# Paired projection: low parts of the weights by accumulating transfers, sums of tokens on VectorE, sums of squares on ScalarE

## The chip, the cores and the metric

One core of one Trainium2 chip runs the kernel. The metric is the time of one execution in microseconds of the device: 2842.64 us is the median of three runs, the lowest 2840.53, the highest 2844.08.

## What is computed

Two layers of a hybrid decoder on a sequence of 1024 tokens with 1024 features, all in float32. In a layer the normalised input goes through one wide projection w_in; its columns feed a retention branch of 4 heads and a gated delta-rule branch of 8 heads, and the gates. Both branches are lifted, gated, added and projected back onto the input.

```python
proj = h @ w_in
qkv = jax.nn.silu(causal_conv(jnp.concatenate([dq, dk, dv], axis=-1), conv_w))
dq = l2norm(dq) * (DN_DK ** -0.5); dk = l2norm(dk)
o_d = gated_deltanet(dq, dk, dv, beta, g)      # chunked, with a triangular solve in each chunk
o_d = o_d * lax.rsqrt(jnp.mean(o_d * o_d, axis=-1, keepdims=True) + EPS) * dn_g
y = jax.nn.sigmoid(gr) * (o_r @ w_up_r) + jax.nn.sigmoid(gd) * (o_d @ w_up_d)
return x + y @ w_o
```

## The kernel before

Each engine has its own instruction stream; they meet in semaphores. A product in float32 is made of three matmuls: every operand is split into a high part, rounded to the matmul's format (tiles `w_hi`, `act_hi`), and a low part, the difference (`w_lo`, `act_lo`); the matmuls are high by high, high by low and low by high. The high part of a weight tile is a copy, its low part the subtraction `w_raw - w_hi`.

A layer begins with one delta unit of kind "first", which prepares the first half of head 0 while TensorE works through whole 128-column blocks of w_in (L1014 to L1018). For heads 0 to 6 follow two units each, "even" and "odd", one for each half of the tokens; then "even_last" and "odd_last" for head 7, the retention heads, the lifting and the output blocks. In a unit the triangular systems are solved by 15 pairs of small VectorE steps on a 16-wide base (L2616, L2619), spread into `xT` (L2626) and doubled three times; beside it the four chunks of the half before run through the state: k times state (PE, L1379), u (VectorE, L2635), v_new (PE L1390, ScalarE L1928), new state (PE L1403, VectorE L2650). The order of all steps is the list that `unit_schedule` writes, one list for all engines; each engine takes its own steps from it, in order. A unit has 24 slots ("first": 36).

In the fourteen even and odd units TensorE's remaining time is filled with 45 pieces a unit of the paired projection (`pair_pieces`, L1216 to L1218). A pair `u` (21 in a layer, three to a head) makes two 128-column blocks at once for all tokens and saves products in the manner of Strassen on the first four of eight row tiles. It takes 30 pieces; a piece is one weight tile by 512 tokens, three matmuls. Nine parts of the weights are needed, each with a high and a low part: X11, X12, X22 (two row tiles, straight from w_in), S1 to S4 (sums and differences of such tiles, computed by GpSimd in place at L3041, L3043, L3050 and L3054), and J1, J2 (four row tiles each, through `w_j`). `PART_AT` gives the piece of the pair at which a part is prepared: ScalarE copies to `w_hi` (L1777), then GpSimd subtracts to `w_lo` (L3045); the product waits for that in `product`. `THIN_FREE` names the product that frees a part's place.

The activations' side of the pair needs four sums of token tiles (`mix`, steps 0 to 13 of a layer: ten sums or differences of 128x1024, L2977, and four low parts, L2981, by GpSimd; the four high parts by ScalarE, L1784). Thirteen steps lie in the first unit, the last at the start of the first even unit.

Sync's queue loads the weights of the pairs (`pair_load`, L868 and L872) when the parts of the pair before are done, and stands in one order with the stores and reloads of the solve's blocks (L844, L852): for the third pair of a head the load of `w_raw` comes behind the blocks of the next odd unit.

The queries' and outputs' sums of squares are made in two instructions: ScalarE squares 128x512 from PSUM (L1923, L1933), VectorE reduces each 128 columns to one (L2549 in step "qe", L2655 in step "og"). On GpSimd there are besides two mask additions a unit (L3062, L3064), the decayed queries (L3075) and small powers (L3069, L3079).

ScalarE prepares a part in these lines, GpSimd behind it:

```python
eng.activation(part_place(part, u, w_hi), part_from[part], ACT.Copy).then_inc(wp_hi.sem, 1)
...
eng.tensor_tensor(part_place(part, u, w_lo), part_from[part], part_place(part, u, w_hi).bitcast(F32),
                  ALU.subtract).then_inc(wp_lo.sem, 1)
```

## Time and profile before

| | |
|---|---|
| median of 3 runs | 2842.64 us |
| profiled execution | 2846.34 us |
| its span, first to last instruction | 2844.5 us |
| mean granted TensorE clock, of full speed | 0.990 |
| PE busy | 2629.5 us |
| PE's weight loads busy | 2193.1 us |
| DVE (VectorE) busy | 1944.0 us |
| ACT (ScalarE) busy | 842.4 us |
| POOL (GpSimd) busy | 1170.1 us |
| share of the DMA engines' time, q1 (Sync) and q10 (ScalarE) | 20.3% and 6.0% |

Busy time is the time in which an engine executes an instruction, not counting waits, branches and the issue of transfers. Engines overlap, so the columns don't add up to the span. An instruction that is held up by another engine's use of the same memory port is counted as busy for all of that time. The chain of work is followed back from the last instruction, at each step to what released it.

### The profile page before, as it was taken

The page shows a single profiled execution, that of the slowest core. Times are in us where ns is not written, and L with a number is a line of the kernel's source. Part 1 is how long each engine was busy: PE and PEld are TensorE (multiplying, and loading weights), DVE is VectorE, ACT ScalarE, POOL GpSimd, SP SyncE. Part 2 cuts the span into 40 slices and gives each one's busy share as a digit, 9 for nine tenths or more (in the row PEclk, how much of TensorE's full clock was granted, in tenths as well). Part 3 has the DMA queues.
Part 4 walks back from the last instruction along what each step waited for, and adds up shares of the span by engine and source line. Part 5 has one row for each costly group of instructions (what it writes and reads, how often), then busy time and mean ns, then how long its engine had stood idle before and what let it go on. Part 6 is the DMA issues. An engine that isn't in the chain of part 4 may idle for free.

```text
span 2844.5 us, 41656 instructions
## 1 busy us (share of the span) xinstructions
PE 2629.5 (92%) x14624; PEld 2193.1 (77%) x14624; DVE 1944.0 (68%) x4054; ACT 842.4 (30%) x1868; POOL 1170.1 (41%) x943
## 2 busy tenths in 40 slices
PE   7888988998889999999988889988988899999998
PEld 5677776777679989888866777776777789998887
DVE  8887878888865555534588788878878655554333
ACT  5334443434322212300133434343433122222001
POOL 5545444554421122434564445544544122224343
PEclk9999999999999999999999999999999999999999
DMA  4212221322231112333522212222221311124244
GB/s 163 83 50 72 61 80 47 85 60 65 60 90 38 45 47 69 112 100 111 162 80 71 80 45 79 61 65 60 71 77 49 90 43 40 39 67 132 93 130 152
DMA packets 296946, 222.07 MB, mean 78 GB/s; under 512 B 33218, under 2 KB 247572, under 8 KB 296484
## 3 DMA queue, kind: packets, MB, share of 16 engines
q1 hardware_dynamic: 264132, 162.22, 20.3%
q10 hardware_dynamic: 32608, 57.19, 6.0%
q8 instruction: 118, 1.93, 0.3%
q14 instruction: 88, 0.72, 0.1%
HBM read 178.40 MB, written 40.96 MB: 77 GB/s over the span
## 4 chain that ended last, share of the span: by engine, by line
PE 63%; DVE 21%; issue 5%; DMA 5%; SPq 3%; ACT 1%; POOL 1%; DVEq 0%; ACTq 0%
PE dense_ps L1014 10%; PE dense_ps L1016 10%; PE dense_ps L1018 10%; DVE arena L2616 5%; DMA w_raw<-in_w_in 4%; DVE arena L2619 3%; PE dense_ps L1216 3%; PE dense_ps L1218 3%; PE dense_ps L1217 3%; PE dense_ps L1038 2%; PE dense_ps L1039 2%; PE dense_ps L1040 2%; PE work L997 2%; SPq L844 2%; PE work L1218 2%
## 5 line engine op out<-in xcount | busy, mean ns | idle before, releaser
L1014 PE MATMUL dense_ps<-act_hi,w_hi 128*128 128x512 f32 x1208 | 487.5, 404 | 5.3 <-POOL w_lo L2915 2.4
L1016 PE MATMUL dense_ps<-act_lo,w_hi 128*128 128x512 f32 x1208 | 475.9, 394 | 0.0
L1018 PE MATMUL dense_ps<-act_hi,w_lo 128*128 128x512 f32 x1208 | 475.7, 394 | 0.0
L2915 POOL TENSOR_TENSOR w_lo<-w_raw,w_hi 128x1024 fp32r<-128x1024 f32 x80 | 203.3, 2541 | 468.2 <-DVE w_hi L2097 448.1
L3045 POOL TENSOR_TENSOR w_lo<-w_raw,w_hi 128x256 fp32r<-128x256 f32 x252 | 205.4, 816 | 394.6 <-ACT w_hi L1777 393.1
L1216 PE MATMUL dense_ps<-act_hi,w_hi 128*128 128x512 f32 x672 | 286.5, 426 | 0.0
L2279 DVE SCALAR_TENSOR_TENSOR arena<-arena,cols 128x512 f32<-128x512 f32 x288 | 279.3, 970 | 8.2
L1014 PEld LDWEIGHTS dense_ps<-act_hi,w_hi 128*128 128x128 f32 x1208 | 230.6, 191 | 54.9 <-issue 5.7
L1018 PEld LDWEIGHTS dense_ps<-act_hi,w_lo 128*128 128x128 f32 x1208 | 229.6, 190 | 50.0
L1218 PE MATMUL dense_ps<-act_hi,w_lo 128*128 128x512 f32 x672 | 264.3, 393 | 0.0
L1217 PE MATMUL dense_ps<-act_lo,w_hi 128*128 128x512 f32 x672 | 264.1, 393 | 0.0
L1016 PEld LDWEIGHTS dense_ps<-act_lo,w_hi 128*128 128x128 f32 x1208 | 230.2, 191 | 42.3 <-issue 0.5
L3045 POOL TENSOR_TENSOR w_lo<-arena,w_hi 128x512 fp32r<-128x512 f32 (+1 forms) x126 | 148.0, 1175 | 120.4 <-ACT w_hi L1777 120.4
L2616 DVE TENSOR_TENSOR arena<-arena 128x60 f32<-128x60 f32 (+14 forms) x480 | 166.2, 346 | 12.3
L1777 ACT ACTIVATE w_hi<-w_raw 128x256 fp32r<-128x256 f32 x252 | 103.7, 412 | 178.2 <-DMA w_raw<-in_w_in 67.6
L1218 PEld LDWEIGHTS dense_ps<-act_hi,w_lo 128*128 128x128 f32 x672 | 126.4, 188 | 28.3
L1216 PEld LDWEIGHTS dense_ps<-act_hi,w_hi 128*128 128x128 f32 x672 | 127.7, 190 | 17.6
L1217 PEld LDWEIGHTS dense_ps<-act_lo,w_hi 128*128 128x128 f32 x672 | 127.6, 190 | 17.7
L1216 PE MATMUL work<-act_hi,w_hi 128*128 128x512 f32 x336 | 139.8, 416 | 0.0
L997 PE MATMUL work<-mk,arena 128*128 128x128 f32 x768 | 115.7, 281 | 25.1 <-DVE arena L2293 17.6
L2619 DVE TENSOR_TENSOR arena<-arena 128x60 f32<-128x60 f32 (+14 forms) x480 | 122.5, 255 | 16.5
L1218 PE MATMUL work<-act_hi,w_lo 128*128 128x512 f32 x336 | 131.8, 392 | 0.0
(320 smaller groups left out, 6157.7 us busy)
## 6 DMA issues: line engine op xcount, KB each, us to landing
w_raw<-in_w_in SPq DMA_DIRECT2D x56, 512.0 KB, 3.8
w_raw<-in_w_in SPq DMA_DIRECT2D x84, 256.0 KB, 3.4
arena<-in_w_in SPq DMA_DIRECT2D x84, 256.0 KB, 2.9
arena<-l_scratch SPq DMA_DIRECT2D x64, 256.0 KB
arena<-gate_scratch ACTq DMA_DIRECT2D x64, 256.0 KB, 2.9
gate_scratch<-arena ACTq DMA_DIRECT2D x36, 256.0 KB, 2.8
w_raw<-in_w_out SPq DMA_DIRECT2D x18, 512.0 KB, 4.2
o_scratch<-arena ACTq DMA_DIRECT2D x32, 256.0 KB, 2.2
```

Of the source, the lines that this page charges most:

```text
L997: mm = eng.transpose(wk[bank][:, c * P:(c + 1) * P], src, ident)
L1014: eng.matmul(dense_ps[:, to, :], w_hi[:, slot, k, :], hi[:, k, seg], start=(k == 0), stop=False)
L1016: eng.matmul(dense_ps[:, to, :], w_hi[:, slot, k, :], lo[:, k, seg], start=False, stop=False)
L1018: mm = eng.matmul(dense_ps[:, to, :], w_lo[:, slot, k, :], hi[:, k, seg], start=False, stop=(k == KT - 1))
L1216: eng.matmul(bank, hi[:, k, :], acts[0][:, k, :], start=first, stop=False, skip_group_check=True)
L1217: eng.matmul(bank, hi[:, k, :], acts[1][:, k, :], start=False, stop=False, skip_group_check=True)
L1218: mm = eng.matmul(bank, lo[:, k, :], acts[0][:, k, :], start=False, stop=last, skip_group_check=True)
L2279: eng.scalar_tensor_tensor(out=acc[:, i % 2, :], in0=src, scalar=wcol, in1=acc[:, i % 2, :], op0=ALU.mult, op1=ALU.add).then_inc(conv_s.se ...
L2616: eng.tensor_tensor(xm[:, :, 0:left], column, xs[:, :, k:k + 1].to_broadcast([P, CPH, left]), ALU.mult).then_inc(sv_s.sem, 1)
L2619: eng.tensor_tensor(xs[:, :, k + 1:BASE], xs[:, :, k + 1:BASE], xm[:, :, 0:left], ALU.add)\
L2915: eng.tensor_tensor(w_lo[:, slot, :, :], w_from[second][:, :, :], w_hi[:, slot, :, :].bitcast(F32), ALU.subtract)\
L3045: eng.tensor_tensor(part_place(part, u, w_lo), part_from[part], part_place(part, u, w_hi).bitcast(F32), ALU.subtract).then_inc(wp_lo.sem, 1)
```

## The change

- The low parts of X11, X12, X22, J1 and J2 are no longer subtracted by GpSimd. ScalarE writes the negated high part into `w_lo` behind the high part (a second copy with scale -1), and GpSimd issues a transfer from w_in in HBM to `w_lo` that adds to what stands there. The product waits for the landing. GpSimd waits before an issue for the transfer before it on the same semaphore (one for the X parts, one for the J parts).
- S1 to S4 are still subtracted by GpSimd. `PART_AT` puts X12, J1, S3, S4, X22 and J2 one to three pieces earlier.
- Sync's pair loads wait for ScalarE's copies (and for the low part of S4) in the place of GpSimd's subtractions.
- All `mix` sums and low parts run on VectorE, in other slots of the first unit.
- The squares are four activations of 128 columns that write their sums; the two reductions fall away.
- The semaphores of the gate loads and the x loads at the end of a layer are merged, so that the first two x loads wait for the last gate loads.

```diff
-PART_AT = (-14, -12, -9, -6, -3, 3, 5, 7, 10)
-PART_NO = {part: i + 1 for i, part in enumerate(PARTS)}
+PART_AT = (-14, -12, -9, -7, -5, 2, 4, 6, 7)
+ADDED_THIN, ADDED_WIDE = ("X11", "X12", "X22"), ("J1", "J2")
+ADDED = ADDED_THIN + ADDED_WIDE
+PART_NO = {part: i + 1 + len([p for p in PARTS[:i + 1] if p in ADDED]) for i, part in enumerate(PARTS)}
...
-        for n in range(9):
-            at(6 + n, "mix", n)
-        for n in range(9, 13):
-            at(13 + n, "mix", n)
+        for n, slot in enumerate((8, 9, 10, 11, 12, 13, 14, 15, 15, 24, 26, 27, 30)):
+            at(slot, "mix", n)
...
+        def added(t, part):
+
+            if part in ADDED_THIN:
+                return thin_in, 16 * (len(ADDED_THIN) * t + ADDED_THIN.index(part) + 1)
+            return wide_in, 16 * (len(ADDED_WIDE) * t + ADDED_WIDE.index(part) + 1)
...
-                            eng.wait_ge(wp_lo.sem, wp_lo.after(t - 1, LOWS["X22"]))
+                            eng.wait_ge(wp_hi.sem, wp_hi.after(t - 1, PART_NO["X22"]))
+                            eng.wait_ge(wp_lo.sem, wp_lo.after(t - 1, LOWS["S4"]))
...
-                        eng.wait_ge(wp_lo.sem, wp_lo.after(t, LOWS["J1"]) if rest else wp_lo.after(t, 0))
+                        eng.wait_ge(wp_hi.sem, wp_hi.after(t, PART_NO["J1"] if rest else 0))
...
-                        eng.wait_ge(wp_lo.sem, wp_lo.after(t, LOWS[part]))
+                        if part in ADDED:
+                            eng.wait_ge(*added(t, part))
+                        else:
+                            eng.wait_ge(wp_lo.sem, wp_lo.after(t, LOWS[part]))
...
+                            if part in ADDED:
+                                eng.wait_ge(wp_hi.sem, wp_hi.after(w, PART_NO[part] - 1))
+                                eng.activation(part_place(part, u, w_lo), part_from[part], ACT.Copy, scale=-1.0)\
+                                   .then_inc(wp_hi.sem, 1)
...
-                            eng.activation(sq, wk[1 + nb][:, :], ACT.Square).then_inc(sq_ok.sem, 1)
+                            for c in range(CPH):
+                                ins = eng.activation(sq[:, c * P:(c + 1) * P], wk[1 + nb][:, c * P:(c + 1) * P], ACT.Square,
+                                                     accum_out=qss[:, c:c + 1])
+                            ins.then_inc(sq_ok.sem, 1)
...
                     if i >= 2:
                         eng.wait_ge(xn_ok.sem, xn_ok.after(l * (NHALF * KT) + i, -1))
+                    else:
+                        eng.wait_ge(xo_in[i].sem, xo_in[i].after(l, 0))
...
-                            eng.tensor_reduce(qss, sq.rearrange("p (c t) -> p c t", c=CPH), mybir.AxisListType.X, ALU.add)\
-                               .then_inc(qe_s.sem, 1)
...
+                            if part in ADDED:
+                                tiles, block = {"X11": (low_k, 0), "X12": (high_k, 0), "X22": (high_k, 1),
+                                                "J1": (slice(CPH, KT), 0), "J2": (slice(CPH, KT), 1)}[part]
+                                done, count = added(w, part)
+                                if count > 16:
+                                    eng.wait_ge(done, count - 16)
+                                eng.dma_start(part_place(part, u, w_lo), w_src(l, w_in, pair_columns(u)[block])[:, tiles, :],
+                                              accum_op=ALU.add).then_inc(done, 16)
+                            else:
+                                eng.tensor_tensor(part_place(part, u, w_lo), part_from[part],
+                                                  part_place(part, u, w_hi).bitcast(F32), ALU.subtract).then_inc(wp_lo.sem, 1)
```

`mix` itself is the same function, moved from the GpSimd stream to the VectorE stream; the squares of the outputs (step "osq", reduction in "og") change as those of the queries do.

## Rows read from the trace of the kernel before

**Rows 1.** The page, part 1: busy us, share of the span, instructions.
```profile
PE 2629.5 (92%) x14624; PEld 2193.1 (77%) x14624; DVE 1944.0 (68%) x4054; ACT 842.4 (30%) x1868; POOL 1170.1 (41%) x943
```
**Rows 2.** Busy time by stretches: PE, PEld, DVE, ACT, POOL, clock, DMA share, GB/s.
```profile
403.00:500.40 97.40, 88.05 (x512) 71.74 (x512) 80.55 (x188) 39.58 (x97) 48.25 (x50) 1.00 0.24 66
...
60.00:104.00 44.00, 27.38 (x117) 21.85 (x116) 41.63 (x65) 13.11 (x28) 29.06 (x13) 0.81 0.26 78
```
**Rows 3.** Who PE waited for, whole span: us in total, times, longest.
```profile
PE work L1390 <- DVE arena L2635: 64.5, 86, 1.5
...
PE work L1379 <- DVE arena L2650: 30.4, 28, 1.3
PE work L1403 <- ACT arena L1928: 25.2, 14, 3.0
```
**Rows 4.** Timeline of DVE and POOL in two solves: start us, us, engine, line.
```profile
424.35 0.79 DVE L2616 TENSOR_TENSOR arena<-arena 128x52 f32<-128x52 f32 x1
...
426.42 1.21 DVE L2616 TENSOR_TENSOR arena<-arena 128x48 f32<-128x48 f32 x1
427.66 0.21 DVE L2619 TENSOR_TENSOR arena<-arena 128x48 f32<-128x48 f32 x1
...
476.05 0.73 DVE L2619 TENSOR_TENSOR arena<-arena 128x52 f32<-128x52 f32 x1
...
480.02 1.28 DVE L2616 TENSOR_TENSOR arena<-arena 128x28 f32<-128x28 f32 x1
...
426.26 1.30 POOL L3045 TENSOR_TENSOR w_lo<-arena,w_hi 128x512 fp32r<-128x512 f32 x1
```
**Rows 5.** The chain of waits in the stretch of one head, its shares by line.
```profile
by line: DVE arena L2616 9.9%; issue 7.0%; PE dense_ps L1216 6.8%; PE dense_ps L1218 6.6%; PE dense_ps L1217 6.6%; DVE arena L2619 6.6%; DMA w_raw<-in_w_in 6.3%; PE work L1218 3.6%; PE work L1216 3.3%; PE work L1217 3.3%; SPq L844 3.0%; PE 
```
**Rows 6.** First unit: DVE by line from 53.7 to 89.7; single steps; POOL.
```profile
L2279 DVE SCALAR_TENSOR_TENSOR arena<-arena,cols 128x512 f32<-128x512 f32 x6 | 13.0, 2160 | 0.1
L2293 DVE SCALAR_TENSOR_TENSOR arena<-arena 128x512 f32<-128x512 f32 x3 | 6.4, 2137 | 0.0
L2276 DVE TENSOR_SCALAR arena<-arena,cols 128x512 f32<-128x512 f32 x2 | 5.2, 2624 | 0.0
L2433 DVE TENSOR_TENSOR arena<-mk,arena 128x512 f32<-128x512 f32 x1 | 2.9, 2922 | 0.0
...
52.23 0.46 DVE L2276 TENSOR_SCALAR arena<-arena,cols 128x512 f32<-128x512 f32 x1
...
99.89 0.74 DVE L2279 SCALAR_TENSOR_TENSOR arena<-arena,cols 128x512 f32<-128x512 f32 x1
...
100.89 0.67 DVE L2433 TENSOR_TENSOR arena<-mk,arena 128x512 f32<-128x512 f32 x1
...
L2103 DVE TENSOR_TENSOR w_lo<-w_raw,w_hi x10: 1217/1226/2332, 40.6 to 2563.3; 128x1024 fp32r<-128x1024 f32 x10
...
L2977 POOL TENSOR_TENSOR arena<-act_hi x4: 2764/2839/2925, 54.7 to 1487.2; 128x1024 f32<-128x1024 f32 x4
```
**Rows 7.** Instructions of two lines: ns shortest/median/longest, first and last start.
```profile
L2655 DVE TENSOR_REDUCE arena<-arena x32: 672/682/689, 148.4 to 2291.1; 128x4 f32<-128x512 f32 x32
...
L1928 ACT ACTIVATE arena<-work x128: 254/277/279, 122.0 to 2286.3; 128x128 f32<-128x128 f32 x128
```
**Rows 8.** The copies to w_hi (as rows 7), and timeline rows of X12.
```profile
L1777 ACT ACTIVATE w_hi<-arena x126: 402/620/634, 112.0 to 2194.6; 128x512 fp32r<-128x512 f32 x84, 128x256 fp32r<-128x256 f32 x42
...
416.11 0.40 ACT L1777 ACTIVATE w_hi<-w_raw 128x256 fp32r<-128x256 f32 x1
...
423.09 0.40 PE L1216 MATMUL dense_ps<-act_hi,w_hi 128*128 128x512 f32 x1
```
**Rows 9.** Issues (KB each, median us to landing), and a load in the chain.
```profile
arena<-in_w_in SPq DMA_DIRECT2D x84, 256.0 KB, 2.9
...
461.99 6.13 DMA w_raw<-in_w_in
```

More of the change, by code:

```diff
@@ L55 @@
 PARTS = ("X11", "S1", "S2", "X12", "J1", "S3", "S4", "X22", "J2")
-PART_AT = (-14, -12, -9, -6, -3, 3, 5, 7, 10)
-PART_NO = {part: i + 1 for i, part in enumerate(PARTS)}
+PART_AT = (-14, -12, -9, -7, -5, 2, 4, 6, 7)
+ADDED_THIN, ADDED_WIDE = ("X11", "X12", "X22"), ("J1", "J2")
+ADDED = ADDED_THIN + ADDED_WIDE
+PART_NO = {part: i + 1 + len([p for p in PARTS[:i + 1] if p in ADDED]) for i, part in enumerate(PARTS)}
 THIN = {"X11": 0, "S1": 1, "S2": 2, "X12": 3, "S3": 4, "S4": 5, "X22": 6}
-LOWS = {step: i + 1 for i, step in enumerate(("sum_S1", "sum_S3", "X11", "sum_S2", "S1", "S2", "X12", "sum_S4", "J1", "S3",
-                                              "S4", "X22", "J2"))}
+LOWS = {step: i + 1 for i, step in enumerate(("sum_S1", "sum_S3", "sum_S2", "S1", "S2", "sum_S4", "S3", "S4"))}
 THIN_FREE = {"X11": (-1, "c11"), "S1": (-1, "p7"), "S2": (-1, "c12"), "X12": (-1, "p4"),
@@ L1930, in delta_unit @@
                             eng.wait_ge(o_ps.sem, o_ps.after(t, CPH))
-                            if kind != "odd_last":
-                                eng.wait_ge(qe_s.sem, qe_s.after(tn, 1))
-                            eng.activation(osq, wk[1 + b][:, :], ACT.Square).then_inc(osq_ok.sem, 1)
+                            eng.wait_ge(og_s.sem, og_s.after(t, 0))
+                            for c in range(CPH):
+                                ins = eng.activation(osq[:, c * P:(c + 1) * P], wk[1 + b][:, c * P:(c + 1) * P], ACT.Square,
+                                                     accum_out=og[:, 0, c:c + 1])
+                            ins.then_inc(osq_ok.sem, 1)
                         elif what == "store":
@@ L2429, in delta_unit @@
                             low_w(g + idx, idx % 2)
+                        elif what == "mix":
+                            mix(step[1])
                         elif what == "mask" and kind == "first":
@@ L3051, in delta_unit @@
                             elif part == "X12":
-                                eng.wait_ge(wp_lo.sem, wp_lo.after(w, LOWS["X12"]))
                                 eng.wait_ge(wp_lo.sem, wp_lo.after(w, LOWS["sum_S2"]))
                                 eng.tensor_tensor(raw_x["X12"], raw_x["X12"], raw_x["X11"], ALU.subtract).then_inc(wp_lo.sem, 1)
-                        elif what == "mix":
-                            mix(step[1])
                         elif what == "mask" and kind != "first":
```

116 lines of the change are left out of this document (55 added, 61 removed).

## The prediction

> **What bounds the kernel now.** I read the page first [rows 1]: TensorE (PE) is busy 92% of the span, VectorE (DVE) 68%, GpSimd (POOL) 41%, ScalarE (ACT) 30%. So the kernel can win only what PE idles, 2844.5 - 2629.5 = 215 us in all. The table by stretches says where that is [rows 2]. One head of the paired stage (the stretch from 403 to 500.4; there are 14 such, seven in each layer) takes 97.4 us with PE busy 88.05 and DVE 80.55: 9.35 us idle, 131 us in 14 heads. In the first unit (60 to 104) PE works 27.4 of 44 us while DVE is busy 41.6: 16.6 us idle, and the second layer has the same unit. The two make 164 of the 215 us. The waits of PE [rows 3] name DVE above all: its u step (L2635) holds the next product 86 times, 64.5 us, its state update (L2650) 28 times, 30.4 us; ACT's v_new copy (L1928) does so 14 times, once a head, 25.2 us.
>
> Why is DVE late? The timeline of the solve in one head [rows 4]: a step on 48 columns takes 0.21 us alone (at 427.66) and 1.21 at 426.42, where it ends together with POOL's low part of J2 (426.26, 1.30 us). The steps at 424.35, 476.05 and 480.02 are stretched in the same way. DVE does not run slowly there, it stands until POOL's subtraction is over. These steps are on the path: in the chain of this head the solve's two lines hold 9.9% + 6.6% = 16.1 us [rows 5]. The first unit is worse [rows 6]: POOL's token sums run back to back at about 2.8 us each, and every two-input DVE step takes the time of one: L2279 2.16 us on average for six, against 0.74 alone.
>
> The Trainium skill says the same in "SBUF — State Buffer", section "Who interferes with whom": a DVE instruction with two SBUF inputs contends with a GpSimd instruction that reads SBUF, and the later one blocks entirely. The trace agrees (1.21 against 0.21 us).
>
> **The token sums (mix, 14 a layer) go from POOL to DVE.** DVE stops being blocked in the first unit, by [rows 6]: six L2279 x (2.16 - 0.74) = 8.5; three L2293 x (2.14 - 0.74, the like form) = 4.2; two L2276 x (2.62 - 0.46) = 4.3; L2433 and another mask like it, 2 x (2.92 - 0.67) = 4.5; one L2103, 2.33 at its longest against 1.23, 1.1. Sum 22.6. DVE takes over 13 sums of 128x1024, each like L2103: 16.0. It must now wait for ACT's high copy at step 12; a 128x1024 copy is about 1.1 us, an estimate from the 128x256 and 128x512 copies (0.40 and 0.62 us, [rows 8]). One reduction of 0.7 goes. Net 22.6 + 0.7 - 16.0 - 1.1 = 6.2. Step 13 stands at the start of the next unit, 1.2 us of work and up to 1.1 of waiting behind ACT's copy, which itself waits for the dense blocks; behind it on DVE is the state copy. Half of that falls in DVE's own wait: 1 us. So -5.2 a layer, **-10 us**; DVE is 95% busy there [rows 2] and PE idles for more, so it is all on the path. Bounds: 0 and -22.
>
> **Low parts of X11, X12, X22, J1, J2.** Five of nine POOL subtractions a pair go; in their place ACT writes a second, negated copy, POOL issues a transfer that adds the weights from HBM, and PE waits for its landing.
> Gain: in the head of [rows 4] the steps held by these parts are J2 1.21 - 0.21 = 1.0, X22 0.79 - 0.23 (the other steps near it) = 0.55, J1 1.28 - 0.2 = 1.1, X12 0.73 - 0.2 = 0.5: 3.1 us a head, 43 us in 14. Nearly all of it is on the chain, but behind DVE's path there is PE's own work and, once a head, a load of 6 us (below), so I take three quarters: **-33 us**. Bounds: 0 (the issue of a transfer holds DVE as the subtraction did) and -43. The subtractions of the S parts, the sums and the decayed queries stay on POOL and go on blocking.
> Cost on ACT: 3 x 0.40 + 2 x 0.62 = 2.4 us a pair [rows 8], 102 us in 42 pairs on an engine 30% busy, so mostly free. Not free is one place a head: ACT stands at the high copy of X11 for the w_raw load (6.13 us from issue, [rows 9]), and v_new, which PE awaits, is queued behind it. A second copy in front of it adds 0.40 x 14 = **+6 us**.
> Cost of lateness: the tightest product I find is X12 of the first pair of a head: copied at 416.11 to 416.51, first used by PE at 423.09 [rows 8]. It now comes one piece earlier, a piece (one weight tile, three matmuls, 90 in a head) being 97.4 / 90 = 1.08 us, less a second copy of 0.40: 6.58 + 1.08 - 0.40 = 7.3 us are left for POOL's issue and the landing. No row shows an accumulating transfer or one issued by POOL. The nearest are SP's loads from the same tensor, 2.9 us to landing in the median, and the pair's load at 6.13 [rows 9]; for the issue I take up to 1.3 us, what the subtraction J2 held POOL. So 4.2 us, in time; at worst 7.4, late by 0.1, and some spread beyond it. I put **+3 us**; ends 0 and +15 (late by 1.1 every head). Four of the five parts have moved ahead by one to three pieces. On POOL's queue the sums for S2 and S4 stand behind an issue, and ACT's copies of S2 and S4 behind them; an issue of up to 1.3 us stands there in the place of a subtraction of 0.7 to 1.3, so nothing is added. POOL's new wait is for the transfer before on the same semaphore, most of a pair earlier: nothing. Traffic grows by 42 x (3 x 128 + 2 x 256) KB = 37.6 MB, hidden at a DMA share of 0.24 [rows 2].
>
> The Trainium skill prices a transfer issued by GpSimd at 2.0 us + bytes / 436e3 ("DMA: Bandwidth & Descriptors", "Anatomy of one DMA"), an estimate of 2.3 us for X12; nothing here shows it, and by it the lateness would be 0 and the sum 3 us lower. Against the change speaks its page "SBUF — State Buffer", "Who interferes with whom": VectorE's copies and tensor_scalars in their two-port mode keep GpSimd from generating descriptors. One such step a conv (L2276) could delay an issue by its own 0.46 us; the room above holds that.
>
> SP's loads now wait for ACT's copies and not for POOL's subtraction, so they start a little sooner; I count nothing, since the one late load of a head waits for the solve's blocks that are stored ahead of it on SP's queue.
>
> **Sums of squares by ACT.** Two reductions of 0.68 us [rows 7] leave DVE in every unit: 28 x 2 x 0.68 = 38 us. Only part is on the path: in the head shown DVE is idle for 16.9 of 97.4 us anyway. I take three tenths, **-11.5 us** (0 to -38). ACT does four squares of 128 columns, near 4 x 0.28 = 1.1 us by its 128x128 copy [rows 7], for one of 512 columns, 0.6 us; each sum may cost an instruction more, which no row shows. DVE's step behind them comes 0.5 us later and 0.68 sooner: even, at worst, with as much again for the sums, 0.9 later.
>
> **Nothing:** the merged gate and x semaphores. ACT waits for the last two gate loads before two x loads, which are not needed before the first output block is done; uncovered it would be a load's 2.9 us a layer [rows 9].
>
> **Sum.** -10 - 33 - 11.5 + 6 + 3 = -45.5 us. The profiled execution took 2846.3 us (span 2844.5), which gives 2800.8; the median shown is 3.7 below it, so **2797 us**.
>
> **Rivals.**
> (a) The issue holds DVE as the subtraction did, because building a transfer of 256 or 512 rows also uses the memory port. Then -33 falls away: 2797 + 33 = 2830. For it: the port is plainly the scarce thing in [rows 4]. Against: an issue reads no tile.
> (b) DVE is the whole bound, and everything it sheds is won: -10 - 43 - 38 + 6 = -85, 2757. For it: the two larger waits of [rows 3] name DVE. Against: DVE itself waits 17% of a head.
> (c) The head is held by the fixed chain of store, reload and the 6.13 us load; DVE's savings in the paired stage only lengthen other waits. Then -10 + 6 are left: 2839, no change that can be told. For it: the 6 us on the chain once a head. Against: the solve's 16 us on it.
> (d) Slower: the added transfers land late. An accumulating transfer reads its target, adds and writes back. If issue and landing take 13 us, X12 is 5.7 us late in each head, 80 us in 14, which gives 2877. It decides from 7.3 + 45.5 / 14 = 10.5 us on. For it: one load here already needs 6.13 us [rows 9]. Against: 10.5 is well above every load of this size in these rows.
>
> **How the numbers follow.** Forecast 0.53, (a) 0.17, (b) 0.10, (c) 0.05, (d) 0.15. A measurement of this kernel can tell about 0.2%, 5.7 us, from no change. The forecast, (b) and most of (a) (0.14) are faster: 0.77. (c) and the rest of (a), where ACT costs more: 0.08 same. (d): 0.15 slower. The range reaches over (b), (a) and (c), from 2750 to 2846, and leaves out (d) and a little below: about 0.18.
>
> **What would show it.** Right: the first unit's DVE steps back at 0.74 us and its PE idle near 11 us; solve steps stretched beside S parts and the decayed queries alone; DVE's busy time down by some 90 us, ACT's up by 130 or more; head near 95 us. Wrong: PE waiting at L1216 for a transfer (d); 1 us solve steps beside a POOL issue (a); the wait of PE for ACT's v_new well over 31 us.

## The result, and the profile of the changed kernel

The changed kernel takes 2937.54 us (median of three, 2936.11 to 2943.68) where the kernel before takes 2842.64. The ratio is 1.034, 95% interval 1.0315 to 1.0365: 95 us slower. The prediction said 2797 us, and with a chance of 0.77 faster. The profiled execution took 2937.54 us itself, with a span of 2935.7.

The page, part 1 and part 4, to be held against [rows 1] and [rows 5]:

```profile
PE 2668.0 (91%) x14624; PEld 2224.7 (76%) x14624; DVE 1893.9 (65%) x4018; ACT 980.4 (33%) x2526; POOL 1118.8 (38%) x915
...
PE 55%; DVE 22%; DMA 9%; issue 7%; ACT 3%; SPq 2%; POOL 1%; DVEq 0%; ACTq 0%; POOLq 0%
```

DVE works 50 us less and POOL 51 less. But PE is "busy" for 38.5 us more with the same 14624 matmuls, so they ran at a lower clock (0.975 granted on average, 0.990 before), and its idle time has gone from 215 to 268 us. Together that is the 91 us of the two spans.

The table by stretches (columns as in [rows 2]): the first unit, and a head of the paired stage.

```profile
60.00:104.00 44.00, 35.79 (x178) 28.57 (x177) 39.60 (x93) 16.01 (x42) 8.72 (x8) 0.92 0.33 94
430.50:533.70 103.20, 89.34 (x506) 72.60 (x505) 78.58 (x183) 48.64 (x138) 49.33 (x49) 0.98 0.46 90
```

In the same 44 us of the first unit PE now does 35.8 us of work in place of 27.4: the token sums won what was hoped. A head takes 103.2 us in place of 97.4 in this pair of windows; from the first product of a head to the first of the next, the median of twelve is 106.4 in place of 98.1. From the first to the last product of the paired stages the two layers take 51.7 and 56.4 us longer, 108 us; 16 us are won in the two first units and 1 behind the last. That is the 91 us, and the question is what happens in a head.

Who PE waited for (us in total, times, longest), and two waits behind which others stand:

```profile
PE work L1401 <- DVE arena L2700: 71.0, 77, 2.1
PE work L1414 <- ACT arena L1945: 70.1, 15, 5.5
PE work L1364 <- DVE arena L2668: 29.0, 16, 2.3
PE dense_ps L1227 <- DMA w_lo<-in_w_in: 15.3, 13, 2.7
...
ACT w_hi L1788 <- DMA w_raw<-in_w_in: 89.6, 14, 6.9
...
DVE arena L2314 <- ACT arena L1654: 103.1, 42, 7.2
```

L1401 is the product that waits for u (L1390 in [rows 3]); L1414 is the state product that waits for ACT's v_new (L1403 there): 25.2 us have become 70.1, once a head, about 5 us each. L1364 is a level of the spread: its wait was 0.8 us before, while that of the level beside it has fallen from 33.9 to 16.5. L1227 waits for added transfers.

The chain of waits through the middle of a head (start us, us, what) shows why v_new is late:

```profile
475.42 0.57 SPq L858
...
476.09 0.41 SPq L875
...
476.54 8.27 DMA w_raw<-in_w_in
484.82 0.42 ACT w_hi L1788
...
485.27 0.02 ACT w_lo L1791
...
485.59 0.16 ACT arena L1654
...
486.11 0.27 ACT arena L1945
...
486.43 0.58 PE work L1414
```

The load of the middle pair is queued on SP behind the blocks of the solve. Its landing releases ACT's copy of X11; the second copy, the tanh and v_new stand behind that on ACT. The load needs 8.27 us, in [rows 9] it was 6.13. PE stands for 4.85 us, and then this happens (timeline of PE):

```profile
486.43 0.79 PE L1414 MATMUL work<-arena 128*128 128x128 f32 x2 [4.85 <-ACT arena L1945]
...
488.58 0.78 PE L1227 MATMUL dense_ps<-act_hi,w_hi 128*128 128x512 f32 x1
489.15 0.51 PE L1228 MATMUL dense_ps<-act_lo,w_hi 128*128 128x512 f32 x1
489.50 0.40 PE L1229 MATMUL dense_ps<-act_hi,w_lo 128*128 128x512 f32 x1
```

A product of 128x512 takes 0.40 us as a rule ([rows 8]) and 0.78 at 488.58. The granted clock of the 4.75 us from 486.36 on is 0.68 on average, between the levels of 1.2 GHz (0.5) and 2.4 GHz (1.0), which is about 3 us at the lower one. I took the mean duration of these products in the 5 us behind the middle v_new of every head: it is above 440 ns in 14 of 14 heads of this kernel, and in 2 of 14 of the kernel before (undisturbed: 407).

The middle v_new is not the only such place. Of the pairs' 128x512 products 116 take over 0.5 us in this kernel (8 in the kernel before), and 71 of them stand elsewhere, for instance behind a wait for u:

```profile
556.91 0.49 PE L1401 MATMUL work<-arena 128*128 128x128 f32 x2 [2.06 <-DVE arena L2700]
...
558.15 0.63 PE L1227 MATMUL work<-act_hi,w_hi 128*128 128x512 f32 x1
```

### The profile page after: what moved, and what is told of

Read it like the earlier page. It is cut to its first block, busy times and chain, and to the rows that moved or that the text cites. A ratio compares the mean times of both kernels' runs of the same rounds, so it can differ in the third digit from the quotient of the medians.

```text
span 2935.7 us, 42416 instructions
## 1 busy us (share of the span) xinstructions
PE 2668.0 (91%) x14624; PEld 2224.7 (76%) x14624; DVE 1893.9 (65%) x4018; ACT 980.4 (33%) x2526; POOL 1118.8 (38%) x915
## 4 chain that ended last, share of the span: by engine, by line
PE 55%; DVE 22%; DMA 9%; issue 7%; ACT 3%; SPq 2%; POOL 1%; DVEq 0%; ACTq 0%; POOLq 0%
PE dense_ps L1022 10%; PE dense_ps L1026 10%; PE dense_ps L1024 10%; DMA w_raw<-in_w_in 4%; DVE arena L2681 3%; DMA w_lo<-in_w_in 3%; DVE arena L2300 2%; PE dense_ps L1046 2%; PE dense_ps L1047 2%; PE dense_ps L1048 2%; DVE arena L2684 2%; DVE arena L2297 2%; PE dense_ps L1227 2%; PE work L1005 2%; SPq L850 2%
## 5 line engine op out<-in xcount | busy, mean ns | idle before, releaser
L3068 POOL DMA_DIRECT2D w_lo<-in_w_in x210 | 277.7, 1322 | 252.6 <-ACT w_lo L1791 232.7
L1227 PE MATMUL dense_ps<-act_hi,w_hi 128*128 128x512 f32 x672 | 294.4, 438 | 15.5 <-DMA w_lo<-in_w_in 15.3
L2300 DVE SCALAR_TENSOR_TENSOR arena<-arena,cols 128x512 f32<-128x512 f32 x288 | 259.2, 900 | 8.0
L3071 POOL TENSOR_TENSOR w_lo<-w_raw,w_hi 128x256 fp32r<-128x256 f32 x126 | 99.4, 788 | 281.9 <-ACT w_hi L1788 280.9
L2681 DVE TENSOR_TENSOR arena<-arena 128x60 f32<-128x60 f32 (+14 forms) x480 | 155.8, 325 | 12.3
L1227 PEld LDWEIGHTS dense_ps<-act_hi,w_hi 128*128 128x128 f32 x672 | 131.4, 196 | 39.4 <-DMA w_lo<-in_w_in 22.0
L1227 PE MATMUL work<-act_hi,w_hi 128*128 128x512 f32 x336 | 142.1, 423 | 0.0
L1228 PE MATMUL work<-act_lo,w_hi 128*128 128x512 f32 x336 | 134.4, 400 | 0.0
L2314 DVE SCALAR_TENSOR_TENSOR arena<-arena 128x512 f32<-128x512 f32 x96 | 66.5, 692 | 105.4 <-ACT arena L1654 103.1
```

The lines of the kernel that those rows point to most:

```text
L1227: eng.matmul(bank, hi[:, k, :], acts[0][:, k, :], start=first, stop=False, skip_group_check=True)
L1228: eng.matmul(bank, hi[:, k, :], acts[1][:, k, :], start=False, stop=False, skip_group_check=True)
L2300: eng.scalar_tensor_tensor(out=acc[:, i % 2, :], in0=src, scalar=wcol, in1=acc[:, i % 2, :], op0=ALU.mult, op1=ALU.add).then_inc(conv_s.se ...
L2681: eng.tensor_tensor(xm[:, :, 0:left], column, xs[:, :, k:k + 1].to_broadcast([P, CPH, left]), ALU.mult).then_inc(sv_s.sem, 1)
L3068: eng.dma_start(part_place(part, u, w_lo), w_src(l, w_in, pair_columns(u)[block])[:, tiles, :], accum_op=ALU.add).then_inc(done, 16)
```

## Experiments

Three edits travel in this change, and the third has parts. All times are medians; "before" was run again with every group and gave 2842.0, 2842.1, 2845.6, 2843.4 and 2846.3 us, so numbers of different groups compare to some 4 us. Every kernel below also has the merged gate and x semaphores. The stretch behind the last paired product, where they act, takes 628 to 632 us in all of them and 631 in the kernel before, so they cost nothing that can be told.

### One edit at a time

**The token sums alone.** Diff of the kernel before:

```diff
-        for n in range(9):
-            at(6 + n, "mix", n)
-        for n in range(9, 13):
-            at(13 + n, "mix", n)
+        for n, slot in enumerate((8, 9, 10, 11, 12, 13, 14, 15, 15, 24, 26, 27, 30)):
+            at(slot, "mix", n)
```

and `mix` moved from POOL's program to DVE's.

> The kernel before with the token sums alone moved from POOL to VectorE, at the changed slots; subtractions, reductions and the parts' places as before. Theory T (the added transfers cost the 95 us, by parts that land late and by traffic): this edit keeps its whole gain, about 8 us a layer at the first unit (the first product of layer 0 was at 118.3 before and at 110.4 in the changed kernel), so about 2827 us against 2843. Theory S (ScalarE's added work costs it): the same here. Theory C (the changed order of the first unit is itself a part of the loss, its gain being lost again in the heads): 2843 or more.

Measured: 2827.1 us, ratio 0.9942 (0.9921 to 0.9964): 15 us, the whole gain that the two first units show.

**The squares' sums alone.** Diff, and the same for the squares of q:

```diff
-                            eng.activation(osq, wk[1 + b][:, :], ACT.Square).then_inc(osq_ok.sem, 1)
+                            for c in range(CPH):
+                                ins = eng.activation(osq[:, c * P:(c + 1) * P], wk[1 + b][:, c * P:(c + 1) * P], ACT.Square,
+                                                     accum_out=og[:, 0, c:c + 1])
...
```

> The kernel before with the squares' sums alone made by ScalarE's accumulation (the two reductions on VectorE gone). Theory T: a small gain or nothing, 2832 to 2846, the reductions' time being off VectorE. Theory S (ScalarE's 1.14 us per set of squares in place of 0.60, in front of the tanh and the v_new copies, and the norm step now meeting POOL's masks) : slower, 16 heads by 2 to 4 us, 2875 to 2905.

Measured: 2846.6 us, 1.0011 (1.0001 to 1.0020): nothing that counts. DVE is busy 36 us less (1944.0 to 1908.0) and nothing is won. Either none of it was on the path, or what was is used up by ACT, whose squares take 1.14 us a set in place of 0.60; no run separates the two.

**The transfers alone**, with the new places of the parts:

```diff
-PART_AT = (-14, -12, -9, -6, -3, 3, 5, 7, 10)
+PART_AT = (-14, -12, -9, -7, -5, 2, 4, 6, 7)
+ADDED_THIN, ADDED_WIDE = ("X11", "X12", "X22"), ("J1", "J2")
```

> The kernel before with the low parts of the five pair blocks made by the second copy and the accumulating transfer, at the changed places of the parts; token sums on POOL and reductions on VectorE as before. Theory T: nearly all of the loss is here, and the gain of the first unit is missing, so about 2937 plus 16 = 2950 (between 2935 and 2965). Theory S: its share is only the five second copies per pair (0.3 to 0.6 us each), under a third of the loss: 2865 to 2885.

Measured: 2959.7 us, 1.0411 (1.0388 to 1.0433).

**Everything but the transfers and the places.**

```diff
-PART_AT = (-14, -12, -9, -7, -5, 2, 4, 6, 7)
-ADDED_THIN, ADDED_WIDE = ("X11", "X12", "X22"), ("J1", "J2")
+PART_AT = (-14, -12, -9, -6, -3, 3, 5, 7, 10)
+ADDED_THIN, ADDED_WIDE = (), ()
```

> The changed kernel with the transfers undone: second copies and transfers gone, the five subtractions back on POOL, the parts' places as before; token sums on VectorE and squares' sums on ScalarE stay. Theory T: faster than before by the sum of the two other edits, 2815 to 2830. Theory S: the squares hold it, 2860 to 2890.

Measured: 2825.3 us, 0.9933 (0.9915 to 0.9951). The time is theory T's: the third edit is the whole loss, 2825 to 2938, and the other two are worth 17 us. What in the third edit costs, T only guessed. This run is the base of all that follow; I call it the base.

### What in the third edit costs

Four kernels take it apart at the new places. Thin parts only:

```diff
-ADDED_THIN, ADDED_WIDE = ("X11", "X12", "X22"), ("J1", "J2")
+ADDED_THIN, ADDED_WIDE = ("X11", "X12", "X22"), ()
```

> The changed kernel with J1 and J2 taken back to copy and POOL subtraction; only the three thin parts (128 KB each) are transferred. Three theories of the transfers' 112 us (2937 against 2825 without them), or some 8 us a head. Landing (the parts come too late, J1 of a head's first pair with 0.0 us to spare): nearly all is gone, 2830 to 2845. Traffic (the second reading slows the loads beside it, the head's own weights first: 8.3 us in place of 6.1): the thin parts are 3 of 7 of the bytes, so 3/7 of 112 stays, about 2873. Copies (ScalarE's second copies): three of five stay, and the thin ones are the short ones, so 2860 to 2880.

Wide parts only:

```diff
-ADDED_THIN, ADDED_WIDE = ("X11", "X12", "X22"), ("J1", "J2")
+ADDED_THIN, ADDED_WIDE = (), ("J1", "J2")
```

> The changed kernel with X11, X12 and X22 taken back to copy and POOL subtraction; only J1 and J2 (256 KB each) are transferred. Landing: nearly all of the loss stays, 2920 to 2937. Traffic: 4/7 of 112, about 2889. Copies: 2885 to 2900.

All five, without accumulation (`w_lo` then holds the raw weights, so this kernel leaves the subtraction out and computes something else, in the same instructions):

```diff
-                                eng.dma_start(part_place(part, u, w_lo), w_src(l, w_in, pair_columns(u)[block])[:, tiles, :],
-                                              accum_op=ALU.add).then_inc(done, 16)
+                                eng.dma_start(part_place(part, u, w_lo), w_src(l, w_in, pair_columns(u)[block])[:, tiles, :]).then_inc(done, 16)
```

> The changed kernel with the same transfers without accumulation (the low part is then the raw weight, so a wrong share of the product is computed, in the same number of instructions; bytes read and written by the cores' queues are as in the changed kernel but for what the adding itself costs). If it is the accumulation that is slow (landing 3.7 and 5.6 us, where a load of 128 KB to 256 KB by SP takes 2.9 and 3.4 in the kernel before), the landings fall to about 3 and 3.5 us and the time to 2850 to 2880. If it is the issue on POOL, the bytes or the copies, it stays at 2920 to 2940.

Second copies without any transfer:

```diff
-ADDED_THIN, ADDED_WIDE = ("X11", "X12", "X22"), ("J1", "J2")
+ADDED_THIN, ADDED_WIDE = (), ()
+TWICE = ("X11", "X12", "X22", "J1", "J2")
...
-                            if part in ADDED:
+                            if part in TWICE:
```

> The changed kernel without any transfer but with ScalarE's five second copies kept: POOL subtracts as before and writes over them, at the changed places of the parts. Copies: most of the loss is here, 2900 or more. Landing and Traffic: 16 heads by 3 times about 1.9 us of copies, mostly beside idle time, 2825 to 2850. The changed places (J2 and X22 due 3 and 1 to 2 slots earlier) are in this run too, and cost at most the same.

Measured: thin 2961.9 us (1.0419), wide 2878.1 (1.0127), plain 2870.3 (1.0097), copies only 2875.3 (1.0104). None of the three theories of this group said that. Wide parts, which I held for the late ones, add 3 us to the copies alone; thin ones alone are worse than all five together; and plain transfers of the same bytes add nothing in sum: PE's wait for v_new grows from 51.4 us with the copies alone to 64.8, and that for the new state falls from 32.4 to 6.9.

The trace of the thin run shows what its time went into, and it is not the landing: no wait of PE for a transfer is among its larger ones, and the middle load takes 6.5 us (median of ten heads; 6.3 in the base). DVE is busy 1971.2 us, 109 more than with the copies alone. In every head one small step of the solve stands beside POOL (timeline of DVE and POOL):

```profile
444.36 1.19 POOL L3086 DMA_DIRECT2D w_lo<-in_w_in  x1 [1.52 <-ACT w_lo L1809]
...
445.04 3.12 DVE L2702 TENSOR_TENSOR arena<-arena 128x44 f32<-128x44 f32 x1
...
445.13 1.74 POOL L3089 TENSOR_TENSOR w_lo<-arena,w_hi 128x512 fp32r<-128x512 f32 x1
...
446.38 1.71 POOL L3119 TENSOR_TENSOR arena<-arena 128x512 f32<-128x512 f32 x1
```

The issue of X22, the subtraction J2 and the decayed queries follow each other on POOL without a gap, and a step of 0.2 us stands for 3.12, in 14 of 14 heads. Two-input steps that stand more than 1.8 us beyond their short time: 44 here, 2 in the base and with the copies alone, 15 with plain transfers, 30 with the wide parts, 22 in the changed kernel.

The issues of the changed kernel and of the plain one (KB each, median us to landing), and their hold of POOL (busy us, mean ns):

```profile
arena<-in_w_in SPq DMA_DIRECT2D x84, 256.0 KB, 4.4
w_lo<-in_w_in POOLq DMA_DIRECT2D x84, 256.0 KB, 5.6
...
w_lo<-in_w_in POOLq DMA_DIRECT2D x126, 128.0 KB, 3.7
...
L3068 POOL DMA_DIRECT2D w_lo<-in_w_in x210 | 277.7, 1322 | 252.6 <-ACT w_lo L1791 232.7 <-DMA w_lo<-in_w_in 11.8 <-issue 8.0
```

```profile
arena<-in_w_in SPq DMA_DIRECT2D x84, 256.0 KB, 3.9
w_lo<-in_w_in POOLq DMA_DIRECT2D x84, 256.0 KB, 4.3
...
w_lo<-in_w_in POOLq DMA_DIRECT2D x126, 128.0 KB, 2.7
...
L3086 POOL DMA_DIRECT2D w_lo<-in_w_in x210 | 159.7, 761 | 247.4 <-ACT w_lo L1809 235.3
```

Accumulation makes a transfer land 1.0 us (128 KB) and 1.3 us (256 KB) later, makes SP's own load of 256 KB 0.5 us slower in the median (4.4 against 3.9; 2.9 in [rows 9]), and holds POOL 0.56 us longer at each issue. The copies-only run left 50 us to explain without any transfer, and it differs from the base by two things.

### Places or copies

The base with the new places and nothing else:

```diff
-PART_AT = (-14, -12, -9, -6, -3, 3, 5, 7, 10)
+PART_AT = (-14, -12, -9, -7, -5, 2, 4, 6, 7)
```

> The run without transfers, with the parts' changed places alone (X12 one slot earlier, J1 two, S3, S4, X22 one and J2 three slots earlier); no second copy, no transfer. Three theories of the 50 us between 2825 (no transfers, old places) and 2875 (second copies kept, changed places). Places: they alone hold v_new's copies back, since copies and subtractions come ahead of them, 2855 to 2875. Copies: ScalarE's second copies do it, 2825 to 2835. Both: about half, 2845 to 2855.

The changed kernel at the old places:

```diff
-PART_AT = (-14, -12, -9, -7, -5, 2, 4, 6, 7)
+PART_AT = (-14, -12, -9, -6, -3, 3, 5, 7, 10)
```

> The changed kernel, transfers and all, with the parts' old places. Places: 30 to 50 us less, 2885 to 2905. Copies and traffic: the loss stays, and J1 and X12 of a head's first pair, copied later, land one to two slots later than they are wanted, 2940 to 2970.

The second copies at the old places, the subtractions kept:

```diff
+TWICE = ("X11", "X12", "X22", "J1", "J2")
```

> Second copies kept and written over by POOL's subtraction, no transfer, the parts' old places. Places: 2825 to 2840. Copies: 2865 to 2875. Both: about 2850.

| | old places | new places |
|---|---|---|
| no copies, no transfers | 2825.3 | 2870.3 |
| second copies | 2830.9 | 2875.3 |
| second copies and transfers | 2909.6 | 2937.5 |

The places alone cost 45 us, the copies 5 to 6 wherever they stand (3 to 5 by the ratios, whose intervals are 4 to 8 us wide to either side), the transfers 79 or 62. The 79 is the loosest: the three runs of the changed kernel at the old places went from 2896 to 2916 us (ratio 1.0222, 1.0182 to 1.0263). How can places cost that much, with every instruction the same? Two stretches around the middle v_new, of the base and then of the kernel with the new places (columns as in [rows 2]; the first line of each is the 5.25 us up to v_new, the second the 4.75 us behind it):

```profile
458.75:464.00 5.25, 2.65 (x12) 1.58 (x11) 2.32 (x5) 1.11 (x5) 0.97 (x2) 1.00 0.87 223
464.00:468.75 4.75, 4.37 (x24) 3.50 (x24) 3.96 (x8) 1.25 (x4) 4.32 (x6) 1.00 0.00 0
```

```profile
462.70:467.95 5.25, 2.49 (x11) 1.44 (x9) 1.04 (x3) 1.09 (x4) 0.96 (x2) 0.96 0.91 218
467.95:472.70 4.75, 4.68 (x21) 4.29 (x22) 2.56 (x5) 1.21 (x4) 3.04 (x4) 0.68 0.00 2
```

The DMA engines are busy for 0.87 of the time in the stretch before v_new; in the head as a whole the share is 0.24 [rows 2]. PE works a little less in the first stretch and gets a mean clock of 0.68 in the second, where the base kept 1.00. By the count described above, the clock falls behind v_new in 11 of 14 heads with the new places and in 4 of 14 of the base. Its waits:

```profile
PE work L1408 <- DVE arena L2733: 45.9, 29, 1.9
...
PE work L1432 <- ACT arena L1963: 37.7, 14, 4.0
```

The base has 32.7 and 24.2 us there (and 62.0 for u, 38.3 here). The wait for the new state (L1408) is a second place where the clock falls, 12 us behind the first, in ten heads; in the base the same wait is 0.92 us in this head and the products behind it keep 0.40:

```profile
480.44 0.46 PE L1408 MATMUL work<-arena 128*128 128x128 f32 x2 [1.91 <-DVE arena L2733]
...
481.62 0.63 PE L1242 MATMUL work<-act_hi,w_hi 128*128 128x512 f32 x1
```

I went through ten heads matmul by matmul: the new places lengthen them by 30.7 us, of which 12.2 are waits and 18.6 longer matmuls. So the larger half of what the places cost is the clock, which falls at two places of a head after waits grown by about 1 us each.

Which places?

```diff
-PART_AT = (-14, -12, -9, -6, -3, 3, 5, 7, 10)
+PART_AT = (-14, -12, -9, -7, -5, 3, 5, 7, 10)
```

> No transfers, token sums on VectorE, squares' sums on ScalarE, and of the changed places only X12's (one slot earlier) and J1's (two). Theory E (the parts of the coming pair, copied on ScalarE and subtracted on POOL two slots earlier, stand ahead of v_new's copies and of VectorE's conv steps): all of the 45 us, 2860 to 2872. Theory L (the late ones, J2 three slots earlier and X22 one: J2's 1.3-us subtraction falls into the solve or the spread): nothing here, 2820 to 2832.

Measured: 2840.6 us (0.9984, 0.9972 to 0.9997): 15 of the 45 us, neither theory (E said all, L nothing). The remaining 30 belong to S3, S4, X22 and J2 together; they were not split further.

### Landing, or the hold of POOL

67 us lie between plain and accumulating transfers (2870 and 2938). The plain kernel with an operation behind each issue:

```diff
+                                at = 2 + len(ADDED) * w + ADDED.index(part)
+                                eng.tensor_tensor(spare[:, at:at + 1], spare[:, 0:1], negh[:, 0:1], ALU.pow)
```

> The changed kernel with plain transfers (a wrong share of the product is computed, as in the plain run before) and behind each issue one operation of POOL on 128x1, about 0.54 us by the 0.70 us of 128x2 and the 1.01 us of 128x4, so that POOL is held as long as by the accumulating issue. Hold: most of the 67 us comes back, 2910 to 2940. Landing: 2868 to 2885.

Measured: 2881.1 us (1.0123, 1.0095 to 1.0151; plain 1.0097, 1.0078 to 1.0117). The filler took 626 ns, a little more than the 561 that were to be imitated:

```profile
L3090 POOL TENSOR_TENSOR spare<-spare,negh 128x1 f32<-128x1 f32 x210 | 131.4, 626 | 4.8
```

By the medians the hold is a sixth of the 67 us, 11; the intervals allow from nothing to a quarter. The rest comes with the later landings or with what they move. Two places of it can be seen. One is J1 of a head's first pair (timeline; the stall of PE stands in brackets):

```profile
431.12 0.63 ACT L1791 ACTIVATE w_lo<-arena 128x512 fp32r<-128x512 f32 x1
...
432.10 1.75 POOL L3068 DMA_DIRECT2D w_lo<-in_w_in  x1
...
439.05 0.49 PE L1227 MATMUL dense_ps<-act_hi,w_hi 128*128 128x512 f32 x1 [0.51 <-DMA w_lo<-in_w_in]
```

Copy, issue and landing take 7.9 us, and PE is there first: 15.3 us of such waits in all, 4.1 in the plain kernel. The other is the middle load, with medians over ten heads of 6.3 us in the base, 7.4 with plain transfers and 8.2 with accumulating ones. The Trainium skill says in "DMA: Bandwidth & Descriptors", section "SWDGE vs HWDGE vs iDMA", that each DMA engine takes turns between the queues that feed it; the slower loads agree with it.

These two are the smaller part. Between the profiles of the plain and the changed kernel (spans of 2871.2 and 2935.7 us) PE's wait for the low parts grows by 11 us and the one for v_new by 5 (64.8 to 70.1), but the one for u by 22 (48.6 to 71.0), that at the spread (L1364) by 9, and PE is busy 13 us more. DVE is busy 37 us more (1857.1 to 1893.9), nearly all of it in steps that stand beside a POOL operation. The wide run says the same: its middle load is slow too (7.6 us in the median of ten heads), PE waits 59.8 us for v_new and the clock falls behind it in 14 of 14 heads, and it takes 2878 us all the same. So a slow middle load alone does not make the loss. Which later landing moves which POOL operation was not tested.

### Which transfers pay

All at the old places, with the token sums on DVE and the squares' sums on ACT. J2 alone:

```diff
-ADDED_THIN, ADDED_WIDE = (), ()
+ADDED_THIN, ADDED_WIDE = (), ("J2",)
```

> Token sums on VectorE and squares' sums on ScalarE, the old places, and of the five transfers J2's alone (5 us or more between landing and use in the changed kernel). If each transfer costs by itself (traffic of the 256 KB, the second copy, the longer way), 2835 to 2850. If only the late ones cost, it is at least as good as the same without it: 2815 to 2826, one POOL subtraction of 1.3 us a pair being gone.

J1 and J2:

```diff
-ADDED_THIN, ADDED_WIDE = (), ()
+ADDED_THIN, ADDED_WIDE = (), ("J1", "J2")
```

> Old places, J1 and J2 transferred, the thin parts subtracted by POOL. If J1 is a cost at the old places (landing 5.6 us after the issue, the part due about 7 us after its copy in a head's first pair): 16 to 42 waits of 1 to 3 us over the run with J2 alone, 2830 to 2850. If the cost lies with the thin parts: 2795 to 2806.

J2 and X22:

```diff
-ADDED_THIN, ADDED_WIDE = (), ()
+ADDED_THIN, ADDED_WIDE = ("X22",), ("J2",)
```

> Old places, J2 and X22 transferred. X22 had 5 us or more to spare in the changed kernel. If lateness is what costs, this is as good as J2 alone or better: 2798 to 2808. If a thin transfer costs by its issue (1.2 us of POOL in place of a subtraction of 0.8) and by its bytes beside the head's own load: 2812 to 2835.

Measured: J2 alone 2805.8 us (0.9879, 0.9847 to 0.9911), J1 and J2 2810.0 (0.9872, 0.9854 to 0.9889), J2 and X22 2862.4 (1.0058, 1.0043 to 1.0073). J2 wins 20 us over the base (15 by the ratios), so the idea of the change is sound where its place allows it. J1 beside it makes no difference that can be told (PE waits 17.1 us for transfers, and other waits are as much shorter). X22 costs 57 us, though PE never waits for it. In that run the middle load lands after 7.1 us in place of 6.1 (medians of ten heads), and PE waits 38.1 us for v_new:

```profile
PE work L1432 <- ACT arena L1963: 38.1, 14, 5.1
```

With X22 by transfer the next pair's load on SP also waits for ACT's second copy in place of POOL's subtraction; no run separates that from the transfer. X22 was then taken out of the middle pair alone, which gives that pair's load its old wait as well:

```diff
+                            if part == "X22" and u % 3 == 1:
+                                eng.tensor_tensor(part_place(part, u, w_lo), part_from[part],
+                                                  part_place(part, u, w_hi).bitcast(F32), ALU.subtract).then_inc(wp_lo.sem, 1)
```

> As the run with J2 and X22 by transfer at the old places (2862), but X22 of each head's middle pair is subtracted by POOL; its second copy stays. Theory M (X22's bytes and its accumulation run beside the load of the head's middle, which lands in 7.1 us in place of 6.1, and v_new, the next pair's sums and the masks follow it): nearly all of the 57 us is gone, 2806 to 2820, and that load lands in 6.1 to 6.4 us again. Theory N (every thin transfer costs alike): a third is gone, 2838 to 2850.

Measured: 2833.7 us (0.9958, 0.9944 to 0.9972). Half of the 57 us is gone, between the two theories. The middle load is back at 6.2 us and the wait for v_new at its old size:

```profile
PE work L1434 <- ACT arena L1965: 19.9, 14, 2.9
```

The other half sits where X22 still goes by transfer. POOL's decayed queries follow X22 in its queue. With J2 alone (timeline of DVE and POOL):

```profile
410.75 0.74 POOL L3089 TENSOR_TENSOR w_lo<-w_raw,w_hi 128x256 fp32r<-128x256 f32 x1 [0.87 <-ACT w_hi L1806]
...
411.44 1.30 POOL L3119 TENSOR_TENSOR arena<-arena 128x512 f32<-128x512 f32 x1
411.59 1.22 DVE L2702 TENSOR_TENSOR arena<-arena 128x52 f32<-128x52 f32 x1
412.84 0.24 DVE L2699 TENSOR_TENSOR arena<-arena 128x48 f32<-128x48 f32 x1
```

and with X22 by transfer:

```profile
416.01 1.23 POOL L3091 DMA_DIRECT2D w_lo<-in_w_in  x1 [1.47 <-ACT w_lo L1811]
416.25 2.40 DVE L2704 TENSOR_TENSOR arena<-arena 128x48 f32<-128x48 f32 x1
416.83 1.75 POOL L3125 TENSOR_TENSOR arena<-arena 128x512 f32<-128x512 f32 x1
```

The issue comes 0.7 us later in the head than the subtraction did (it waits for the second copy) and takes POOL 1.23 us, so the decayed queries end 1.2 us later, and the solve step next to them takes 2.40 us where 0.2 is its own. It began 0.58 us before the record of the decayed queries does, while the issue was under way, and so in all 14 heads (0.56 to 0.73 us). The head's first masks start 1.4 us later too. Summed over the run, by the POOL operation that a DVE step stands beside the longest, what the steps take beyond their short time is 38 us at the decayed queries (22 with J2 alone) and 51 at the two mask additions (39). Steps that stand over 1.8 us longer are 30 in place of 2, and DVE is busy 28.6 us more; PE's waits for u, for the new state and at the spread are 30 us longer together. That is the other half.

**The reductions again**, on the version with J2:

```diff
-                                ins = eng.activation(osq[:, c * P:(c + 1) * P], wk[1 + b][:, c * P:(c + 1) * P], ACT.Square,
-                                                     accum_out=og[:, 0, c:c + 1])
...
+                            eng.activation(osq, wk[1 + b][:, :], ACT.Square).then_inc(osq_ok.sem, 1)
```

> Token sums on VectorE, J2 by transfer, the old places, and the squares' sums back on VectorE's two reductions. Squares cost nothing either way: 2800 to 2812 (2806 with them on ScalarE). If the reductions' 11 us on VectorE count again now that POOL's subtraction is gone: 2810 to 2825.

Measured: 2815.2 us (0.9894, 0.9869 to 0.9919), against 2805.8 (0.9879) in another group. The intervals overlap: no difference is shown.

## Why the prediction was wrong

**The token sums: -10 us, measured -15** (2842.0 to 2827.1), within the bounds. The first product of the paired stage starts at 111.1 us, 7.2 earlier than before.

**The solve freed of subtractions: -33 us for all five.** The mechanism is there: J2, which I held for a third of it (1.0 of 3.1 us a head), won 20 us net of its second copy. My share for it was 11 us of the 33, so this term was low for J2 and, for X22 and the thin parts, of the wrong sign: the issue does not leave DVE free where POOL has an operation directly behind it (below). DVE's busy time fell by 50 us and not by the 90 that I had named as a sign.

**Squares: -11.5 us, measured 0** (+4.6 with an interval that begins at +0.3; -2 beside the token sums). Of my two bounds, 0 and -38, the first was right. I had taken three tenths of DVE's saving with no row that says which tenths are on the path.

**ACT's second copies: +6 us, measured +5 and +6.** The size came out, the place only in part, and that is luck: at the old places PE's wait for v_new, where I had put all of it, is shorter with the copies (24.2 to 16.9 us) and the loss lies elsewhere; at the new places that wait grows (37.7 to 51.4).

**The first failed step: "Four of the five parts have moved ahead by one to three pieces", costed at nothing.** It is 45 us: in ten heads 12 us of longer waits and 19 of longer matmuls. I had checked whether room was left for the transfers, and not what stands behind each part on ACT and POOL at the new place. A wait that grows by 1 us tips the clock after the middle v_new in 11 heads in place of 4, and a second one, for the new state, in ten.

**The second failed step: the lateness of +3 us, with "Traffic ... hidden at a DMA share of 0.24".** The transfers cost 62 us at the new places, 79 at the old. Two things were wrong in it. The tightest part was not X12 (7.3 us of room; it landed 4.2 us after the issue) but J1 of a head's first pair, which I did not look up. And the share of 0.24 was the mean of a head; in the 5 us where the chain hangs on a load it is 0.87, and there the added bytes make the load take 8.2 us in place of 6.3. The bounds of the landing itself held in the medians (3.7 and 5.6 us against 2.9 at best and 6.13 at worst).

**The third failed step: an issue "stands there in the place of a subtraction ... so nothing is added" on POOL's queue.** The issue waits for a second copy and ends later than the subtraction did, and what POOL runs directly behind it then stands beside the solve. With X22 of the outer pairs and its second copies this is 28 us (2805.8 to 2833.7; 22 by the ratios), with the thin parts alone at the new places DVE is busy 109 us longer than with the copies alone, and the time is 87 us longer.

**What the sum had no term for: the clock.** I took PE's 2629.5 us as fixed and asked only for its idle time. PE is busy 38.5 us more with the same matmuls, two fifths of the 91.

**The rivals.** (d) had the right side and place in part: transfers land late. But its mechanism, X12 late by a landing of 13 us, is not what happened; 15.3 us of PE's waits name a transfer, of 95 lost. (a) is wrong for the issue alone: 337 DVE steps of the changed kernel stand beside an issue with nothing else on POOL, and they are 1 ns longer than alone on average, 10 at most. It is right in part where an operation follows directly: then steps that begin while the issue is under way do stand (25 of 50 such in the changed kernel, and the steps of 2.40 us above), and the records do not tell whether the issue or the operation behind it holds them. (b) fell with the squares, 36 us less on DVE for nothing. (c) said that the fixed chain of store, reload and load hides DVE's savings. It does not: J2's saving was won. But a delay on that chain costs, and I had asked only what gains it hides. The sign I set down for "wrong", a wait for v_new well over 31 us, is what the profile shows, 70.1 us.

The ledger, each from the medians: 2842 before; token sums -15; squares -2; places +45; second copies +5; transfers without accumulation -5; accumulation +67; 2937 in sum, 2937.5 measured. The terms are differences along one chain of runs, so that they add up proves nothing; each is good to some 4 us.

The best median is that of the token sums on DVE, the squares on ACT, the old places and J2 alone by an accumulating transfer: 2805.8 us, 1.2% below the kernel before. J1 in addition (2810.0) and the squares' reductions back on DVE (2815.2) cannot be told from it.

## What to carry to other kernels

Find the one load, or the one copy behind it, on which the slowest chain of a stage hangs, and read the DMA share and the queues in the few microseconds around it, not over the stage: work that is free on average can cost there. Look in the same way at what stands directly behind an instruction that you replace on its own engine, and at which steps of other engines it will then stand beside. Change places and mechanisms in separate steps, since moving an instruction by a slot or two can cost more than the instruction. And where a change sheds an engine's work in several spots, try each alone; here one of five transfers carried the gain and another lost nearly three times as much.

## What the runs showed of the hardware that I had not expected

- An accumulating transfer from POOL lands 1.0 us (128 KB) and 1.3 us (256 KB) later than the same one without accumulation, and its issue takes POOL 1.32 us in place of 0.76.
- The issue does not hold DVE's steps by itself (1 ns on average over 337 of them, 310 with two inputs). With a POOL operation directly behind the issue, DVE steps stand from within the issue to that operation's end: 2.40 us in place of 0.2 in 14 of 14 heads, and 3.12 us where two operations follow.
- The clock falls after small waits: after a stand of 4.85 us PE's 128x512 products took 0.78 us for one and 0.51 for the next before they were back at 0.40, and with stands of 4.4 to 5.5 us this happened in 14 of 14 heads. In the kernel before, the base and the kernel with the new places the stands at this point were 0.5 to 4.0 us, and it came in 2, 4 and 11 of 14.
- Each accumulated sum on ACT is an instruction of its own, 0.21 us, half hidden beside the next square:

```profile
L1938 ACT ACTIVATE arena<-work 128x128 f32<-128x128 f32 x128 | 33.4, 279 | 2.9 <-PE work L1005 2.8
L1938 ACT ACTIVATION_READ_ACCUMULATOR arena<-work 128x1 f32 x128 | 27.0, 211 | 0.0
```
